# Dilated attention of the prompt: keys by remainder and one softmax for three groups, in one inference step of a hybrid sparse decoder

## The chip, the cores and the metric

One Trainium2 chip, one of its cores. The metric is the device time of one execution of the whole program, in microseconds; lower is better. The five engines of the core are TensorE (PE in the profile; PEld are its weight loads), VectorE (DVE), ScalarE (ACT), GpSimd (POOL) and SyncE (SP), which here only issues DMA transfers.

## What is computed

One layer over a prompt of 512 tokens and a sample group of 8 sequences with 4 new tokens each and 2048 tokens of past: RMS norm, one wide projection, two attention mixers, a gated merge, a mixture of experts. The change is in the second mixer for the prompt, dilated attention with three groups of four heads of 64:

```python
DIL_CONFIGS = ((128, 1), (512, 4), (2048, 16))     # (window, dilation)

def dilated_prompt(q, k, v, window, dil):           # per group; residues() sorts tokens by position % dil
    span = window // dil
    ...
    mask = (m_k >= 0) & (diff >= 0) & (diff <= span)
    p, lse = masked_softmax(s, mask)
    o = jnp.einsum('brnhqk,brnkhe->brnqhe', p, vw)

def combine_dilations(outs, lses):
    w = jax.nn.softmax(jnp.stack(lses, axis=-1), axis=-1)
    o = jnp.einsum('bthn,bthnd->bthd', w, jnp.stack(outs, axis=-2))
```

A query of group 0 reads itself and the 128 keys behind it, one of group 1 every 4th key behind it, one of group 2 every 16th. The three outputs of a head are weighted by a softmax over the groups' log denominators. That is the same as one softmax over the keys of all three groups together.

The outputs also hold the updated window caches: for the sample group each is the old cache moved on by four tokens (a copy from HBM to HBM, here called a cache move) with the new rows at its end.

## The kernel before

The program is a sequence of blocks; each is a list of instructions per engine, ordered by semaphores, and a block begins when the one before has ended on all engines.

- `norm_and_project` (L180): projection. A loop of turns takes two chunks of 328 columns of the weights. `load` (L217) loads a chunk on SyncE when TensorE has finished with its buffer, VectorE splits it in two parts, TensorE multiplies. The loop on SyncE (L223) has four turns of two loads.
- `finish_rows` (L429): merge gates, rotary embedding, compressor. SyncE stores the rows of keys and values to the prompt's caches (`put`, L476) and issues the eight moves of the 512 cache.
- `prompt_nsa` (L777): the first mixer for the prompt, 32 steps of scores, maximum, exponential, turned probabilities, values. SyncE issues two moves of the 2048 cache (4088 KB each) when each of four head pairs begins, and at the end waits until the rows are stored (L967).
- `prompt_dilated` (L1119): the block that changes. 24 steps: 2 head pairs x 4 tiles of 128 queries x 3 groups. `step(k)` (L1134) gives the key blocks of a step: up to 2 for group 0, all up to the diagonal for groups 1 and 2, whose masks (`dil1`, `dil2`) cross out keys with another remainder. `scores` (L1224) forms queries x keys and adds the mask with a product of the identity in bf16 (L1238); `maxima` on VectorE (L1367), `exps` on ScalarE (L1314). When the three groups of a unit have their exponentials, `max_differences`, `group_factors` and `weights` work out one factor for each group and GpSimd multiplies the exponentials (L1209). `turn_probs` transposes them (L1250), `copy_pT` on VectorE (L1388) and ScalarE (L1329) brings them to SBUF, `values` (L1263) multiplies: the values (64 columns) are the stationary operand and 128 queries stream, so the output comes out turned and `copy_o` (L1393) stores it. TensorE's order in iteration k is scores of k + 6, probabilities of k + 1, values of k. Ahead of the loop six turns bring queries and keys of the first pair (L1216); `turn_next` does it for the second. `sample_queries` and `sample_keys_and_gates` prepare the next block within the last four steps.
- On SyncE this block issues the loads of group 1's cached keys and values (g1) for the next block, then, when each head pair begins, four moves of the 128 cache (248 KB each) and four of the window cache (508 KB each), then the first window keys (`load_first_window_keys`, L1471), whose place is in `rows`.
- `sample_dilated` (L1496): the same mixer for the sample group; it begins with g1 and the first window keys. Then come `sample_nsa`, `mix` and `experts`.

An f32 product appears as two MATMUL instructions with a weight load each, a transpose or a bf16 product as one.

## Time and profile before

| what | us |
|---|---|
| three runs, median (lowest to highest) | 1165.11 (1160.56 to 1166.38) |
| profiled execution, span | 1161.6 |
| TensorE busy | 1055.2 (91%) |
| VectorE, ScalarE, GpSimd busy | 501.6, 331.2, 175.6 |
| block of `prompt_nsa` | about 305 to 406 |
| block of `prompt_dilated` | about 406 to 477 |
| `sample_dilated` begins | 478 |
| expert weights in the chain that ended last | 9.5% of the span |

For the profiled execution the page gives the span, from the first to the last instruction; it lies within the three runs. The span is cut in 40 slices of 29 us; TensorE is at 9 tenths in most, the DMA engines above 9 tenths in the last nine but two. A busy TensorE is not one at its peak: pipelined products overlap, and what a group of products costs is read from the starts of the groups. In every view times count from the start of the span.

### The profile page before, as it was taken

To read this page: it belongs to the slowest core of one execution; us is meant where nothing else is said; L and a number is where in the kernel's file an instruction comes from. 1 tells how busy PE (TensorE), PEld (TensorE's weight loads), DVE (VectorE), ACT (ScalarE), POOL (GpSimd) and SP (SyncE) were. 2 spreads that over 40 slices of the span, in tenths; PEclk is the share of its full clock that TensorE was granted. 3 is DMA by queue.
4 is the path that set the end of the run, shared out by engine and by line. 5 is a ranking of instruction groups with operands and counts; after the bars stand their busy time and mean duration, and the time that the engine had idled before them with its cause. 6 is when DMAs were issued, how large, how long until landed. Compare 5 with 4: busy or idle time off the path is not lost. (4 is left out here: it accounts for less than half of the span.)

```text
span 1161.6 us, 20328 instructions
## 1 busy us (share of the span) xinstructions
PE 1055.2 (91%) x8174; PEld 780.8 (67%) x8176; DVE 501.6 (43%) x1065; ACT 331.2 (29%) x766; POOL 175.6 (15%) x212
## 2 busy tenths in 40 slices
PE   6999999999889979886999999999997999888785
PEld 6999999999856646765887887887555433333332
DVE  5444343333367668643656657526216211100105
ACT  4100001221346556422555454520111111100103
POOL 0260000500035534201010010000000112011200
PEclk9999999999869999997999999999998999898989
DMA  8421250887379997497555343409916899999966
GB/s 259 130 90 55 87 147 14 230 307 262 139 254 348 326 307 248 132 340 238 229 198 209 146 171 148 159 1 335 419 69 261 304 425 421 422 424 425 424 258 248
DMA packets 99119, 279.05 MB, mean 240 GB/s; under 512 B 17540, under 2 KB 72736, under 8 KB 87648
## 3 DMA queue, kind: packets, MB, share of 16 engines
q1 hardware_dynamic: 88992, 228.72, 54.7%
q0 software_dynamic: 6976, 42.48, 9.6%
q10 hardware_dynamic: 3072, 6.75, 1.5%
q8 instruction: 55, 0.90, 0.3%
q14 instruction: 24, 0.20, 0.1%
HBM read 263.67 MB, written 69.53 MB: 287 GB/s over the span
## 5 line engine op out<-in xcount | busy, mean ns | idle before, releaser
L3100 PE MATMUL ex_up_ps<-ex_w_up,ex_hT 128*64 128x512 f32 x512 | 123.5, 638 | 27.1 <-DMA ex_w_up<-in_expert_w_up 25.5
L123 PE MATMUL proj_acc<-w_in_upper,hT_upper 128*128 128x328 f32 x352 | 112.3, 319 | 2.6 <-DVE hT_rest L117 2.3
L125 PE MATMUL proj_acc<-w_in_upper,hT_rest 128*128 128x328 f32 x352 | 110.5, 314 | 0.0
L3100 PEld LDWEIGHTS ex_up_ps<-ex_w_up,ex_hT 128*64 128x64 f32 x512 | 41.6, 146 | 97.6 <-issue 86.7
L124 PE MATMUL proj_acc<-w_in_rest,hT_upper 128*128 128x328 f32 x252 | 79.8, 316 | 0.0
L123 PE MATMUL sn_hp<-sn_xT,cmp_w_upper 128*128 128x256 f32 x256 | 76.4, 298 | 0.0
L123 PE MATMUL proj_acc<-hT_upper,merge_w_upper 128*128 128x272 f32 x256 | 74.3, 290 | 1.3 <-ACT qT_dil L557 1.3
L124 PE MATMUL proj_acc<-hT_rest,merge_w_upper 128*128 128x272 f32 x256 | 73.7, 288 | 0.0
L125 PE MATMUL proj_acc<-hT_upper,merge_w_rest 128*128 128x272 f32 x256 | 73.5, 287 | 0.0
L124 PE MATMUL sn_hp<-sn_xT,cmp_w_upper 128*128 128x256 f32 x256 | 73.1, 286 | 0.0
L125 PE MATMUL sn_hp<-sn_xT,cmp_w_rest 128*128 128x256 f32 x256 | 73.1, 285 | 0.0
L123 PEld LDWEIGHTS proj_acc<-w_in_upper,hT_upper 128*128 128x128 f32 x352 | 66.7, 189 | 4.5 <-DVE hT_rest L117 2.7
L3254 DVE TENSOR_TENSOR ex_act<-ex_silu,ex_up_ps 128x256 f32<-128x256 f32 x16 | 6.7, 420 | 144.9 <-ACT ex_silu L3190 144.9
L125 PEld LDWEIGHTS proj_acc<-w_in_upper,hT_rest 128*128 128x128 f32 x352 | 66.7, 190 | 0.0
L3123 PE MATMUL ex_down_ps<-ex_w_down,ex_actT 128*64 128x512 f32 x256 | 58.4, 597 | 2.1 <-DMA ex_w_down<-in_expert_w_down 1.4
L123 PEld LDWEIGHTS sn_hp<-sn_xT,cmp_w_upper 128*128 128x128 f32 x256 | 49.3, 193 | 2.2 <-issue 1.9
L1838 POOL DMA_INDIRECT sn_raw<-in_cache_nsa_paged,page_rows x16 | 17.4, 1090 | 215.6 <-ACT sn_v L2233 148.7
L124 PEld LDWEIGHTS sn_hp<-sn_xT,cmp_w_upper 128*128 128x128 f32 x256 | 49.4, 193 | 0.0
L125 PEld LDWEIGHTS sn_hp<-sn_xT,cmp_w_rest 128*128 128x128 f32 x256 | 49.3, 193 | 0.0
L123 PEld LDWEIGHTS proj_acc<-hT_upper,merge_w_upper 128*128 128x128 f32 x256 | 48.1, 188 | 1.7 <-ACT qT_dil L557 1.5
L2199 ACT CAST sn_xT<-sn_tp 128x512 fp32r<-128x512 f32 x64 | 34.3, 591 | 51.7 <-PE sn_tp L2034 41.4
L977 POOL TENSOR_TENSOR qrot_and_spare<-qrot_and_spare,pn_stats 128x256 f32<-128x256 f32 (+3 forms) x32 | 40.1, 1253 | 55.8 <-DVE pn_stats L1045 55.8
(530 smaller groups left out, 2125.7 us busy)
## 6 DMA issues: line engine op xcount, KB each, us to landing
ex_w_up<-in_expert_w_up SPq DMA_DIRECT2D x30, 2048.0 KB, 29.5
ex_w_down<-in_expert_w_down SPq DMA_DIRECT2D x32, 1024.0 KB, 30.1
out_dil_sample<-in_cache_dil_w SPq DMA_DIRECT2D x8, 4088.0 KB, 27.8
sd_kv_g<-in_cache_dil_w SPq DMA_DIRECT2D x32, 512.0 KB, 7.6
w_in_chunk<-in_w_in SPq DMA_DIRECT2D x10, 1312.0 KB, 5.9
merge_w<-in_w_in SPq DMA_DIRECT2D x16, 512.0 KB, 5.7
out_dil_sample<-in_cache_dil_w SPq DMA_DIRECT2D x8, 1016.0 KB, 8.5
merge_gates_scratch<-qT_dil ACTq DMA_DIRECT2D x16, 272.0 KB, 4.5
```

The costliest lines, as they stand in the source:

```text
L123: pe.matmul(out, a[0], b[0], start=first, stop=False)
L124: pe.matmul(out, a[0], b[1], start=False, stop=False)
L125: return pe.matmul(out, a[1], b[0], start=False, stop=last)
L977: pool.tensor_tensor(part, part, bc(st[:, k % 8, 3, :], 2, [P, 2, n]), ALU.mult).then_inc(s_sc, 1)
L1838: pool.indirect_dma_start(self.sn_raw[:, g % RAW].rearrange("c p x -> c (p x)"), None, half, bass.IndirectOffsetOnAxis(ap=self.page_rows[: ...
L2199: act.copy(xT[:, x_units_to(u) % XR, 0, :, bank, 0:P], a[bank][:, :].rearrange("p (j c) -> p j c", j=4)).then_inc(s_ea, 1)
L3100: ins = pe.matmul(up_ps[r, q, :], hT[:, q, c, r], wu[slot][:, u, c, :], start=c == 0, stop=c == KD - 1)
L3123: ins = pe.matmul(dn_ps[r, half, :], aT[:, q, c, r], wd[slot][:, u, c, half * 512:(half + 1) * 512], start=c == 0, stop=c == 1)
L3254: dve.tensor_tensor(ac[:, q, :], sl[:, q, :], up_ps[:, q, FF:2 * FF], ALU.mult).then_inc(s_ac, 1)
```

## The change

- Queries of a tile are ordered by position modulo 4 (`RES`), so 32 queries (`RQ`) have one remainder. For groups 1 and 2 each of the four sets of 32 queries is multiplied with the keys of its own remainder only: (i + 1) x 32 keys for tile i instead of (i + 1) x 128. Group 2 keeps a mask for its steps of 4 within them.
- The scores of all three groups of a unit lie side by side in one PSUM bank per head, at most 256 + 2 x 128 columns, and one maximum, one exponential and one sum serve them all. The factors, the differences and GpSimd's multiplications are gone. There are 8 units instead of 24 steps.
- In `values` the probabilities become the stationary operand and 64 value columns stream. The output comes out with queries as rows: `normalize` divides it by the sum, `turn_output` transposes it, `copy_o` stores it in the old order.
- Groups 1 and 2 need values by remainder; `prompt_nsa` loads them back from the stored caches into `v_turned`, on SyncE ahead of the 2048 moves, after a wait for the stored rows and the turned queries.
- The moves of the 128 cache and the window cache go from this block to the loop of the projection, two of each per turn.
- The sample's copies on ScalarE and VectorE go behind the loop; the mask table shrinks from 1536 to 1152 columns.

```diff
+RES, RQ = 4, P // 4
@@ norm_and_project, SyncE
                         load(0, i + 1)
                         load(1, i + 1)
+                        for j in range(2):
+                            for src, dst in (("cache_nsa_win", "nsa_win_sample"), ("cache_dil_w128", "dil128_sample")):
+                                self.move_cache(sp, src, dst, 2 * i + j)
@@ prompt_nsa, SyncE
+                    sp.wait_ge(s_qt, PAIRS)
+                    sp.wait_ge(self.s_rows_out, 16 * self.n_rows_out)
+                    for g in range(2):
+                        stored = self.o[f"dil{WINDOWS[1 + g]}_prompt"][0, 0].rearrange("(j r) x h d -> j r x (h d)", r=RES)
+                        sp.dma_start(v_turned[:, g], stored[:, :, 1, :]).then_inc(self.s_vt, 16)
                     for c in range(PAIRS):
                         sp.wait_ge(s_s, U * c + 1)
...
-                    sp.wait_ge(self.s_rows_out, 16 * self.n_rows_out)
@@ prompt_dilated, SyncE
-                    for c in range(PAIRS):
-                        sp.wait_ge(s_s, U * c + 1)
-                        for j in range(BS // PAIRS):
-                            for src, dst in (("cache_dil_w128", "dil128_sample"), ("cache_nsa_win", "nsa_win_sample")):
-                                self.move_cache(sp, src, dst, BS // PAIRS * c + j)
+                    sp.wait_ge(s_s, NT + 1)
                     self.load_first_window_keys(sp)
@@ GpSimd
-                    for k in range(N):
-                        c, i, g, kb, n = step(k)
-                        pool.wait_ge(s_co, k // 3 + 1)
-                        part = ex[:, k % EX, :, 0:n]
-                        pool.tensor_tensor(part, part, bc(st[:, k // 3 % 4, 4, g, :], 2, [P, 2, n]), ALU.mult).then_inc(s_sc, 1)
@@ TensorE
+                    def scores(u):
+                        c, i, kb, n0, m = unit(u)
...
+                        heads = [slice(hh * HD, (hh + 1) * HD) for hh in range(2)]
+                        for hh, r in enumerate(heads):
+                            pe.matmul(S[u % 2][:, hh, 0:n0], qT(c, 0)[r, i * P:(i + 1) * P], kT[r, c, 0, k0:k0 + n0], start=True, stop=False)
+                        for g in (1, 2):
+                            at = n0 + (g - 1) * m
+                            for res in range(RES):
+                                q0 = i * P + res * RQ
+                                for hh, r in enumerate(heads):
+                                    pe.matmul(S[u % 2][res * RQ:(res + 1) * RQ, hh, at:at + m], qT(c, g)[r, q0:q0 + RQ],
+                                              kT[r, c, g, res * P:res * P + m], start=False, stop=False)
+                        near, strided = self.mask("near"), self.mask("strided")
+                        s0 = RQ * i * (i + 1)
+                        for hh in range(2):
+                            pe.matmul(S[u % 2][:, hh, 0:n0], self.ident_b[:, :], near[:, 2 * P - n0:2 * P], start=False, stop=False)
+                            ins = pe.matmul(S[u % 2][:, hh, n0:n0 + 2 * m], self.ident_b[:, :], strided[:, s0:s0 + 2 * m], start=False, stop=True)
...
+                    def values(u):
...
+                        for hh in range(2):
...
+                            for a, b in enumerate(kb):
+                                pe.matmul(O[u % 2][:, hh, :], pT[:, u % 2, 0, hh, a * P:(a + 1) * P], rows[:, b, v:v + HD], start=a == 0, stop=False)
+                            for g in range(2):
+                                for res in range(RES):
+                                    at = g * P + res * RQ
+                                    ins = pe.matmul(O[u % 2][res * RQ:(res + 1) * RQ, hh, :], pT[0:m, u % 2, 1, hh, at:at + RQ],
+                                                    v_turned[0:m, g, res, h * HD:(h + 1) * HD], start=False, stop=g == 1)
...
+                    for u in range(-2, N):
+                        if u + 2 < N:
+                            scores(u + 2)
+                        if u >= 1:
+                            turn_output(u - 1)
+                        if 0 <= u + 1 < N:
+                            turn_probs(u + 1)
+                        if u == N - 1:
                             sample_queries()
...
+                        if u >= 0:
+                            values(u)
+                        if 0 <= u + 1 < 3:
+                            turn_next(u + 1)
+                    turn_output(N - 1)
```

## Rows read from the trace of the kernel before

**Rows 1.** Which piece of the chain that ended last: start us, us, what

```profile
966.80 33.52 DMA ex_w_up<-in_expert_w_up
```

**Rows 2.** Windows: us, busy us by engine (x instructions), granted clock, DMA share, GB/s

```profile
320.00:325.00 5.00, 5.00 (x38) 3.74 (x36) 1.82 (x3) 0.00 (x0) 0.00 (x0) 0.50 1.24 422
...
340.00:345.00 5.00, 5.00 (x46) 2.81 (x40) 4.20 (x12) 3.54 (x10) 2.77 (x3) 1.00 0.01 3
...
405.00:420.00 15.00, 10.56 (x87) 6.72 (x84) 9.34 (x30) 7.73 (x32) 5.09 (x10) 1.00 0.99 332
...
440.00:460.00 20.00, 19.61 (x175) 12.25 (x175) 15.40 (x48) 12.41 (x48) 9.80 (x10) 1.00 0.83 267
...
460.00:480.00 20.00, 16.71 (x180) 13.14 (x178) 13.27 (x36) 9.97 (x34) 10.21 (x8) 1.00 0.01 3
```

**Rows 3.** Timeline at both ends of the dilated block: start us, us, engine, line

```profile
409.25 0.49 PE L1234 MATMUL pd_S<-qrot_and_spare,rows 64*128 64x128 f32 x4
...
409.36 0.58 ACT L1344 COPY qrot_and_spare<-pd_O 128x512 f32<-128x512 f32 x1 [0.29 <-PE pd_O L1216]
...
476.05 0.22 DVE L1415 TENSOR_REDUCE gate_rows<-sq_gates 128x6 f32<-128x48 f32 x1
```

**Rows 4.** Timeline of TensorE in a dense stretch of the dilated block

```profile
442.78 0.70 PE L1234 MATMUL pd_S<-qrot_and_spare,rows 64*128 64x256 f32 x4
443.42 0.39 PE L1238 MATMUL pd_S<-masks_bf,ident_bf 128*128 128x256 bf16 x2
443.64 1.04 PE L1250 MATMUL pd_PT<-ident,pd_exp 128*128 128x128 f32 x8
444.61 0.66 PE L1263 MATMUL pd_O<-qrot_and_spare,rows 128*64 128x128 f32 x8
445.20 0.70 PE L1234 MATMUL pd_S<-qrot_and_spare,rows 64*128 64x256 f32 x4
...
447.03 1.09 PE L1263 MATMUL pd_O<-qrot_and_spare,rows 128*64 128x128 f32 x16
448.05 0.70 PE L1234 MATMUL pd_S<-qrot_and_spare,rows 64*128 64x256 f32 x4
```

**Rows 5.** Timeline of TensorE, groups with few weight columns or few streamed, later blocks

```profile
486.31 1.08 PE L1630 MATMUL sd_Sd<-sd_kT,sd_qTz 128*32 128x128 f32 x32
...
502.91 1.42 PE L1600 MATMUL sd_Sd<-sample_place,qT_dil 128*128 128x32 f32 x12
...
512.28 0.40 PE L1670 MATMUL sd_O<-sample_place,sd_pTn 32*32 32x128 f32 x8
...
639.84 2.38 PE L2096 MATMUL sn_misc<-sn_v,sn_pT 128*32 128x128 f32 x40
```

**Rows 6.** Groups by line, 405 to 480 us: busy us, mean ns, idle before

```profile
L1209 POOL TENSOR_TENSOR pd_exp<-pd_exp,pd_stats 128x512 f32<-128x512 f32 x10 | 10.2, 1039 | 27.0 <-DVE pd_stats L1381 27.0
...
L1367 DVE TENSOR_REDUCE pd_stats<-pd_S 128x2 f32<-128x1024 f32 x4 | 4.9, 1220 | 1.1 <-PE pd_S L1238 1.0
```

**Rows 7.** Timeline of SyncE's DMA issues: start us, us, line, transfer

```profile
66.24 64.11 SPq L219 DMA_DIRECT2D w_in_chunk<-in_w_in  x5
...
275.35 2.15 SPq L478 DMA_DIRECT2D out_dil_sample<-rows  x3
...
406.46 24.84 SPq L1494 DMA_DIRECT2D sd_kv_g<-in_cache_dil_w  x8
...
442.62 11.85 SPq L1476 DMA_DIRECT2D rows<-in_cache_nsa_win  x4
```

**Rows 8.** Timeline of VectorE in the projection

```profile
88.05 1.53 DVE L113 CAST w_in_upper<-w_in_chunk 128x2624 fp32r<-128x2624 f32 x1 [4.87 <-DMA w_in_chunk<-in_w_in]
...
91.39 1.17 DVE L117 TENSOR_TENSOR w_in_rest<-w_in_chunk,w_in_upper 128x984 fp32r<-128x984 f32 x1
```

**Rows 9.** DMA issues by line: count, KB each, median us to landing

```profile
out_nsa_win_sample<-in_cache_nsa_win SPq DMA_DIRECT2D x8, 508.0 KB, 9.0
```

**Rows 10.** Waits of SyncE: who waited for whom, us in total, times, longest

```profile
SPq L649 <- PE pn_S L868: 68.2, 4, 29.8
```

## What the change was predicted to do

> **What bounds the kernel now.** I read the chain of work that ended last first. It reaches back only to 882.87 us and from 966.8 us on it is mostly expert weights in transit [rows 1]; nothing in it lies in the stage that changes. But that stage is one link of a sequence of blocks, and the transfers that end the kernel are issued in buffers that come free only after the blocks before. So I take a microsecond saved in the dilated block as a microsecond saved at the end, unless a transfer that the next block needs isn't there. Second, the windows [rows 2]: in 440 to 460 us TensorE is busy 19.6 of 20 us, VectorE 15.4, ScalarE 12.4, GpSimd 9.8. So this block is TensorE's when it is full, and it is not full at its start: 10.6 of 15 us from 405 to 420. Third, the block's ends [rows 3]: first scores at 409.25, last step (the gates) over at 476.3 us.
>
> **What TensorE's work costs.** The dense stretch [rows 4] gives each group by start-to-start. Scores of 256 keys: 0.64 us. Masks of 256: 0.22 for two, nothing lost before the transposes. Eight transposes: 0.97. Value products: 8 instructions 0.59, 16 instructions 1.02, so 54 ns per instruction of 128 columns plus 0.15 per group. 54 ns is 128 columns at about one a cycle of 2.4 GHz. So the 0.64 is 4 instructions x 107 ns plus 0.21, and a transpose is some 0.105 with 0.13 per group. A step with n key blocks costs 0.49 + 0.75n. Before has 24 steps with 54 key blocks: 24 x 0.49 + 54 x 0.75 = 52.3 us.
>
> After has 8 units. An f32 product is two instructions, and the kinds are these:
> - Near scores, masks, transposes (6 in the first unit of a head pair, 8 in the others) and the turn of the output (one transpose, 0.1) go by the prices above.
> - Scores by remainder: 16 products with 32 query columns, 32 instructions per unit, over 32, 64, 96 or 128 keys.
> - Near values now load 128 weight columns and stream 64. The nearest row is L1600 (128 columns loaded, 32 streamed): 12 instructions in 1.42 us, 0.114 us each [rows 5]. So 0.46 us per head with two key blocks, where the old form took 0.22.
> - Values by remainder: 16 products, 32 instructions per unit, 32 weight columns, 64 streamed.
>
> The price of those 512 small instructions isn't in the trace, and it is the largest unknown. Rows with 32 weight columns [rows 5]: L1630, rotating over four column groups, 26 ns at 128 columns streamed (1.08 us less 0.27 for the last one, by 31); L1670, 19 ns; L2096, with two groups taking turns, 54 ns, which is its stream. The values rotate over four groups like L1630, so 27 ns. The scores use two heads on one group before they move on, like L2096, so I take the larger of 27 ns and their stream: 27, 27, 33 (partly overlapped), 40 ns by unit. Bounds: 19 ns and 54 ns.
>
> Unit by unit (near scores + remainder scores + masks + output turn + transposes + values): first 0.42 + 1.07 + 0.24 + 0.1 + 0.8 + 1.9 = 4.6; second 0.64 + 1.07 + 0.34 + 0.1 + 1.0 + 2.4 = 5.6; third 0.64 + 1.27 + 0.39 + 0.1 + 0.9 + 2.4 = 5.7; fourth 0.64 + 1.49 + 0.44 + 0.1 + 0.8 + 2.4 = 5.9. (Values: per head 0.46 near + 0.15 + 16 x 27 ns + 0.15; 0.23 near in the first unit. The 0.2 more in the transposes of the first two is for outputs narrower than the array.) Sum 21.8, both pairs 43.5 us. So TensorE's own work falls by 8.8 us only: three groups of steps are gone, but the remaining keys come in small pieces.
>
> **The waits.** Before, the loop takes 66.3 us (409.25 to 475.6) with 52.3 of this work and 4.9 of turns for the second pair and for the sample (same in both), so 9.1 us are stalls, nearly all in the slow filling seen in rows 2. They come from the combination of groups: a unit's probabilities can't be turned until three steps of exponentials, the factors and GpSimd's multiplications are through. After, a unit needs one maximum (up to 1.22 us, [rows 6]) and two exponentials, and GpSimd's 24 multiplications (1.0 us each at 512, [rows 6]) are gone; they were beside TensorE and are worth only the fill. Following the new order by hand, the first unit waits some 1 us for its exponentials and 1 us for the copies before the next turn; I take 3.5 us. So 5.6 us saved. Against it: the first scores wait for the copies of all three groups, 409.9 instead of 409.25 (ScalarE's third copy starts at 409.36 and takes 0.58, [rows 3]), 0.7 us; and the tail now multiplies, turns and copies after the last product, 0.9 us more. The sample's copies move behind the loop but run beside the last values. VectorE per unit: 1.22 + 0.2 maxima, about 0.5 normalizing, 0.3 output copy, 0.7 probability copy, 2.9 us against 5.9 of TensorE; ScalarE about 2.1. Both are hidden.
>
> 8.8 + 5.6 - 0.7 - 0.9 = 12.8, **13 us saved**.
>
> **The transfers.** The next block needs its first keys. SyncE issues the g1 loads from 406.5 to 431.3 and the first window keys from 442.6 to 454.5 [rows 7], behind 6.3 MB of small cache moves. The DMA engines rest from 460 on (share 0.01, [rows 2]). With the moves gone, the window keys are issued when the fifth unit is scored (near 432), and the work left in the queue, about 1 MB behind g1, lands near 440, while the block now ends at 463. Hidden, with 20 us to spare. The new value loads (1 MB) wait on SyncE in front of the 4 MB cache moves: for stores that were issued by 277.5 us [rows 7] and for the queries to be turned, which the moves wait for in any case. They delay the first moves by about 3 us (1 MB at the 320 GB/s of the stage), which the hole at 340 to 345 us (DMA share 0.01) absorbs [rows 2].
>
> The small moves (8 of 508 KB [rows 9] and 8 of 248 KB) go behind a weight load in the projection: 1.5 MB in each of four turns, about 5 us. They stand on SyncE ahead of the next turn's loads, whose turn comes 16 us later. Loads are issued every 16 us (five issues from 66.24 to 130.35, [rows 7]), so one goes out near 82.3; it has landed at 88.05 and is split by 92.6 [rows 8], and its chunk begins near 98. So there are 5 us of slack even if the moves shared the engines with the load ahead of them. Cost 0; 0 to 4 us as bounds, none of it likely. The smaller mask table saves nothing, TensorE doesn't wait there.
>
> **A rule that speaks against the change.** The group overhead of 0.15 to 0.21 us in rows 4 appears wherever the shape of the array's use changes; before that is 3 times in each of 24 steps, after 6 or 7 times in each of 8 units, so 72 against about 54. The Trainium skill says the same of the cause (TensorEngine Tiling (Array Packing), Key Properties: changing the tiling mode drains the engine), and the new unit switches back and forth between heads in its values. The overhead is in my sum.
>
> **Rivals.**
> - The small pieces run at the two-group pace everywhere. 54 ns for all 512 instead of 29 on average is +12.6 us: no gain, 1165. Against it: the values rotate like L1630.
> - The small pieces overlap fully. A unit uses eight different places of the array (two halves of its rows, four quarters of its columns). Were all eight streaming at once, an instruction would cost an eighth of 54 ns, 7 ns: 512 x 22 ns = 11 us more, 24 saved, 1141. The rows speak against it: four groups give 26 and 19 ns, not 13 or less [rows 5]. By the Trainium skill (TensorE: Matmul & The Clock Gate, Part 3, The mechanism) tiles in different places start about 4 ns apart; by that rule the pieces would be as cheap as in this rival; the trace doesn't agree for f32 products.
> - The stalls stay. If the fill and the alternation of engines cost 9 us as before, the saving is 7: 1158.
> - Slower: the clock. The granted clock is 0.50, which is the lower level of 1.2 GHz, in 320 to 325 us, after a block's start with gaps [rows 2]. The first head pair of the attention before, of which two thirds lie in that stretch, kept SyncE waiting 29.8 us; the other three waits sum to 38.4, of which one is the short first, so 19 us for a later pair [rows 10]. Two thirds at the lower level cost a half more, so the whole some 70%. The loop's 52 us would be some 35 longer: 1165 - 13 + 35 = 1187. It decides from a third of the loop at the lower level (13 of 35). For it: the new loop also begins with gaps, and no row shows pieces of 64 x 32 in a long series. Against it: the old fill had TensorE busy 10.6 of 15 us and kept 1.00 [rows 2], and the new one has fewer gaps.
>
> **How the numbers follow.** The profiled execution spans 1161.6 us, the three runs are 1160.56 to 1166.38 with median 1165.11; I subtract from the median: 1165.1 - 13 = 1152. Chances: forecast (8 to 17 saved) 0.60, stalls stay 0.13, two-group pace 0.12, full overlap 0.05, half clock 0.10. Within 0.5% is 5.8 us, which is about what a measurement of this kernel can tell from no change. Faster: 0.60 + 0.05 + half of the stalls case = 0.70. Same: the other half, most of the two-group case: 0.18. Slower: 0.12. The range holds forecast, stalls and two-group cases, and at the low end 19 ns pieces (-5 us) and the spread of runs (3 us): 1144 to 1167.
>
> **What would show it.** In the profile after: the dilated block from about 406 to 463 us instead of 476. Groups of 32 instructions of 32 columns in about 1.1 us (right) or 1.9 (two-group pace). Near values at 0.11 us an instruction. First value products near 420 us. The window keys land before 445 us. The projection's windows still 20.00 of 20. Granted clock 1.00 in the block. The expert stage as long as before. I am wrong if small instructions cost 50 ns, if a clock below 1 stands in the block, or if TensorE waits for keys behind it.

## The result and the profile after

The changed kernel takes 1146.07 us in the median of 4 executions (1142.88 to 1149.66) against 1165.13 us of the kernel before (1160.56 to 1166.38, 4): the ratio is 0.9846 with a 95% interval of 0.9825 to 0.9867, so it is 19 us or 1.5% faster. In later comparisons the same two kernels stood at 0.9837 (0.9791 to 0.9883), 0.9828 (0.9791 to 0.9865) and 0.9828 (0.9798 to 0.9859). Over all 20 executions of the changed kernel the median is 1145.8 us, and they lie between 1139.94 and 1151.17. The first four runs of before lie within 6 us, but all its 48, with those of the later comparisons, spread as widely, from 1160.12 to 1173.26 (9 to 13 us on each of the later chips); so the 11 us of the changed kernel are not by themselves a sign of the change. What they come from is asked below.

The profiled execution took 1149.66 us, of which the span is 1147.8; it is the slowest of its four. Its chain of work that ended last is of the same kind as [rows 1] (start, us, what):

```profile
966.23 37.83 DMA ex_w_up<-in_expert_w_up
```

The windows that answer [rows 2], with those between 420 and 440 us added (us, busy us of TensorE, its weight loads, VectorE, ScalarE, GpSimd with counts, then granted clock, DMA share, GB/s):

```profile
320.00:325.00 5.00, 5.00 (x34) 3.40 (x32) 2.16 (x3) 0.00 (x0) 0.00 (x0) 0.50 1.04 399
340.00:345.00 5.00, 5.00 (x50) 3.03 (x46) 4.20 (x12) 3.85 (x10) 3.36 (x2) 1.00 0.63 213
405.00:420.00 15.00, 11.74 (x210) 9.35 (x209) 7.43 (x15) 6.81 (x18) 3.33 (x7) 1.00 0.95 317
420.00:425.00 5.00, 3.10 (x50) 2.16 (x48) 1.61 (x4) 0.61 (x2) 0.00 (x0) 0.94 0.89 289
425.00:430.00 5.00, 5.00 (x50) 4.41 (x49) 1.81 (x4) 1.92 (x5) 0.00 (x0) 0.50 1.07 346
430.00:435.00 5.00, 4.23 (x53) 3.57 (x53) 2.07 (x6) 0.58 (x1) 0.00 (x0) 0.50 0.70 224
435.00:440.00 5.00, 5.00 (x79) 3.69 (x77) 1.05 (x3) 1.40 (x5) 0.00 (x0) 0.50 0.74 207
...
440.00:460.00 20.00, 19.04 (x341) 15.77 (x325) 11.19 (x35) 8.47 (x28) 0.00 (x0) 0.93 0.01 3
460.00:480.00 20.00, 15.47 (x167) 13.03 (x167) 11.05 (x30) 5.91 (x15) 2.69 (x2) 0.78 0.57 171
```

GpSimd is out of the loop, VectorE and ScalarE have become lighter, and the block is TensorE's. But the granted clock, which the forecast had at 1.00 all through the block, is at 0.50 (the lower level, 1.2 GHz) in three windows on end. The ends of the block, for [rows 3]:

```profile
409.29 0.49 PE L1232 MATMUL pd_S<-qrot_and_spare,rows 64*128 64x128 f32 x4 [0.77 <-ACT qrot_and_spare L1355]
...
462.43 0.22 DVE L1433 TENSOR_REDUCE gate_rows<-sq_gates 128x6 f32<-128x48 f32 x1
```

The gates end at 462.65 instead of 476.27: 13.6 us earlier. So this one execution shows just the saving that was forecast, with a clock that wasn't. A second profile of the same kernel (run e1) shows the block with no such stretch. Its gates are at 453.00, 23 us earlier than before, and its span is 1140.4 us. Here is its dense stretch at full clock, for [rows 4] (start us, us, engine, line, shapes, count):

```profile
437.99 0.70 PE L1232 MATMUL pd_S<-qrot_and_spare,rows 64*128 64x256 f32 x4
438.62 0.67 PE L1238 MATMUL pd_S<-qrot_and_spare,rows 64*32 64x128 f32 x32
439.22 0.28 PE L1243 MATMUL pd_S<-masks_bf,ident_bf 128*128 128x256 bf16 x1
...
439.67 0.27 PE L1286 MATMUL pd_O<-ident,pd_o_rows 128*128 128x128 f32 x1
439.77 0.38 PE L1258 MATMUL pd_PT<-ident,pd_exp 128*128 128x128 f32 x2
...
440.65 0.56 PE L1276 MATMUL pd_O<-rows,pd_pT 128*128 128x64 f32 x4
441.13 0.43 PE L1280 MATMUL pd_O<-qrot_and_spare,pd_pT 64*32 64x64 f32 x16
441.49 0.66 PE L1276 MATMUL pd_O<-rows,pd_pT 128*128 128x64 f32 x4
442.08 0.43 PE L1280 MATMUL pd_O<-qrot_and_spare,pd_pT 64*32 64x64 f32 x16
```

L1232 are the near scores, L1238 the scores by remainder, L1243 the masks (with L1244, not shown), L1286 the turn of the output, L1258 and L1260 (not shown) the transposes, L1276 the near values, L1280 the values by remainder. By start-to-start, the 32 instructions of L1238 over 128 keys take 0.60 us, or 19 ns each, where 40 were forecast. (Instructions are counted here, two to each f32 product.) The 16 of L1280 take 0.36 us, or 22 ns, where 27 and a group overhead were. Scores over 32, 64 and 96 keys take 0.29, 0.39 and 0.50 us: 9, 12 and 16 ns.

The maxima of VectorE in the whole block, for [rows 6] (the multiplications of GpSimd are gone):

```profile
L1387 DVE TENSOR_REDUCE pd_stats<-pd_S 128x2 f32<-128x384 f32 (+3 forms) x8 | 7.7, 957 | 14.7 <-PE pd_S L1244 14.7
```

SyncE in the changed kernel, for [rows 7]; the small moves now stand between the weight loads of the projection:

```profile
83.61 0.55 SPq L653 DMA_DIRECT2D out_nsa_win_sample<-in_cache_nsa_win  x1
...
98.84 16.32 SPq L220 DMA_DIRECT2D w_in_chunk<-in_w_in  x2
...
405.67 22.42 SPq L1509 DMA_DIRECT2D sd_kv_g<-in_cache_dil_w  x8
433.49 2.68 SPq L1491 DMA_DIRECT2D rows<-in_cache_nsa_win  x4
```

### The profile page after: what moved, and what is told of

It is laid out like the page before. It is cut to its first block and busy times, and to the rows that moved or that the text cites. A ratio compares the mean times of both kernels' runs of the same rounds, so it can differ in the third digit from the quotient of the medians.

```text
span 1147.8 us, 20576 instructions
## 1 busy us (share of the span) xinstructions
PE 1046.5 (91%) x8408; PEld 782.3 (68%) x8408; DVE 476.7 (42%) x985; ACT 310.8 (27%) x678; POOL 148.2 (13%) x188
## 5 line engine op out<-in xcount | busy, mean ns | idle before, releaser
L125 PE MATMUL sn_hp<-sn_xT,cmp_w_upper 128*128 128x256 f32 x256 | 72.5, 283 | 0.0
L126 PEld LDWEIGHTS proj_acc<-hT_upper,merge_w_rest 128*128 128x128 f32 x256 | 48.3, 189 | 0.0
L125 PEld LDWEIGHTS proj_acc<-hT_rest,merge_w_upper 128*128 128x128 f32 x256 | 48.1, 188 | 0.0
L125 PEld LDWEIGHTS proj_acc<-w_in_rest,hT_upper 128*128 128x128 f32 x252 | 48.1, 191 | 0.0
```

The costliest lines, as they stand in the source:

```text
L125: pe.matmul(out, a[0], b[1], start=False, stop=False)
L126: return pe.matmul(out, a[1], b[0], start=False, stop=last)
```

## The experiments

To compare profiles I use three marks in each: the last output copy of the attention before (`oT<-pn_O`), the gates (`gate_rows`), and the start of the last group of the product `sd_tq<-sample_place,sd_o`, near the end of the block that follows. The marks of before, the last of each kind:

```profile
405.90 0.29 DVE L1064 COPY oT<-pn_O 128x128 f32<-128x128 f32 x1 [0.92 <-PE pn_O L935]
...
546.17 1.03 PE L1681 MATMUL sd_tq<-sample_place,sd_o 128*128 128x16 f32 x4 [1.39 <-DVE sd_o L1800]
```

With the gates of [rows 3] at 476.05 the dilated block is 70.2 us long in before, the next block 70.1, and the rest, which is the span behind the third mark, 615.4. A pause is idle time of TensorE in front of a product in the dilated block which waited for nothing that the profile shows ("issue"); only those over 0.3 us are listed.

| run | executions | median us (range) | ratio to before (95%) | dilated block | pauses, us | next block | rest |
|---|---|---|---|---|---|---|---|
| changed kernel, first profile | 4 | 1146.07 (1142.88-1149.66) | 0.9846 (0.9825-0.9867) | 57.3 | 0.92, 1.90 | 70.2 | 615.1 |
| e1 changed kernel | 4 | 1144.32 (1142.25-1149.93) | 0.9837 (0.9791-0.9883) | 47.4 | none | 71.2 | 616.2 |
| e10 changed kernel | 6 | 1143.58 (1139.94-1151.17) | 0.9828 (0.9791-0.9865) | 49.0 | 0.75 | 71.3 | 615.3 |
| e12 changed kernel | 6 | 1147.74 (1140.65-1150.75) | 0.9828 (0.9798-0.9859) | 53.0 | 1.79 | 71.1 | 618.6 |
| e2 moves back | 4 | 1147.55 (1144.65-1154.97) | 0.984 (0.9799-0.9882) | 56.6 | 3.44, 1.76 | 72.5 | 618.8 |
| e3 before, moves only | 10 | 1163.67 (1159.66-1169.22) | 0.9988 (0.9967-1.001) | 70.2 | none | 69.7 | 615.6 |
| e4 no 2048 moves | 4 | 1141.08 (1138.9-1142.19) | 0.9793 (0.9754-0.9832) | 46.9 | none | 71.5 | 613.7 |
| e5 busy end | 5 | 1146.08 (1142.16-1148.04) | 0.9817 (0.9789-0.9845) | 52.3 | 2.32, 0.75 | 70.9 | 616.0 |
| e6 late moves | 5 | 1145.88 (1144.74-1146.72) | 0.9828 (0.9805-0.985) | 48.0 | none | 74.5 | 613.7 |
| e7 heads outer | 4 | 1144.81 (1144.22-1146.63) | 0.9814 (0.9788-0.984) | 49.8 | 0.94 | 73.0 | 615.9 |
| e8 scores twice | 4 | 1154.94 (1151.81-1157.26) | 0.9909 (0.9882-0.9937) | 59.3 | 2.43, 1.92, 0.80 | 70.5 | 614.3 |
| e9 early moves | 6 | 1140.62 (1139.67-1143.88) | 0.9801 (0.9771-0.983) | 47.7 | none | 72.8 | 613.7 |
| e11 early moves | 5 | 1141.93 (1140.1-1143.54) | 0.979 (0.9764-0.9816) | 46.9 | none | 72.1 | 616.6 |

e1 to e4 ran on one chip, e5 to e8 on another, e9 with e10, and e11 with e12. A comparison within a group needs no detour over the kernel before. The changed kernel did not run beside e5 to e8. The rest lies between 613.7 and 618.8 us, so some 5 us of a profile's time come from behind the two blocks; what makes them is not shown. Behind each median stand 4 to 10 executions, behind each row of blocks and pauses one.

### e1: the changed kernel again

> The changed kernel once more, unaltered. Theory: 13.6 us of the saving are made in the dilated block (ends 462.65 instead of 476.3 in its first profile) and the rest is spread between runs, so the time is 1143 to 1150, 15 to 22 below before, and the profile shows again a stretch of 10 to 20 us at granted clock 0.50 between 415 and 445 us and two pauses of 0.9 and 1.9 us inside the remainder scores. Rival: the stretch at 0.50 and the pauses are chance, and a second profile shows 1.00 from 405 to 455 and the block ending near 452, with a time near 1137.

The rival came true for the profile, and the theory for the time: this execution has no pause and no stretch at the lower clock, and its block is 47.4 us. The other three are at 1142.56, 1146.09 and 1149.93 us. So the first profile is not what the kernel always does, and what has to be explained is a difference between executions of one program.

### e2 and e3: the small cache moves

e2 is the changed kernel with the moves back in the dilated block; e3 is the kernel before with nothing but the moves changed. The diff is that of e2 in the dilated block, where the same moves leave the projection.

```
-                    sp.wait_ge(s_s, NT + 1)
+                    for c in range(PAIRS):
+                        sp.wait_ge(s_s, NT * c + 1)
+                        for j in range(BS // PAIRS):
+                            for src, dst in (("cache_dil_w128", "dil128_sample"), ("cache_nsa_win", "nsa_win_sample")):
+                                self.move_cache(sp, src, dst, BS // PAIRS * c + j)
```

> The new attention with the small cache moves put back into the dilated block. Theory (moves cost nothing in the projection, and in the block they only delay the window keys, of which the block has 20 us to spare): within 3 us of the changed kernel, and TensorE's pauses in the fill stay as they are. Rival: the gain beyond the 13 us forecast comes from the transfers taken out of the block; then it is 5 us or more slower than the changed kernel, and the next block waits for its keys.

> The kernel before with the small cache moves alone put into the projection. Theory: within 1 us of before, projection windows still 20.00 of 20 busy, all of the saving belongs to the attention. Rival: the moves are worth 4 to 6 us by themselves (the part of 19 that 13 doesn't explain), so 1159 to 1161.

e3: 0.9988 with 1 inside the interval, so the moves alone bring 1.4 us with bounds of 4 and -1, and the gain is the attention's. e2 is 3.2 us above e1, with intervals that cover each other; the limit of 3 us in the expectation was missed by a hair. Its profile has the longest pause of all, 3.44 us, and a second of 1.76 in the last unit, behind the same 21st of 32 instructions as the pause of e10 in the table; the expectation saw neither coming.

```profile
446.77 0.44 PE L1239 MATMUL pd_S<-qrot_and_spare,rows 64*32 64x128 f32 x11 [1.76 <-issue]
```

With the transfers back, more of them are queued while the block runs (DMA share 0.92 to 1.05 from 440 to 450 us, where the changed kernel has 0.02).

### e4: without the moves of the 2048 group

```
-                    for c in range(PAIRS):
-                        sp.wait_ge(s_s, U * c + 1)
-                        for j in range(BS // PAIRS):
-                            self.move_cache(sp, "cache_dil_w2048", "dil2048_sample", BS // PAIRS * c + j)
```

> The changed kernel without the cache moves of the 2048 group (32 MB less traffic; that output is left out). It asks what makes the two pauses inside the remainder scores and the fall of the clock behind them. Theory: the pauses are the fetch of instructions (a 16 KB instruction packet lies at 409 and at 420 us, where the pauses are) behind the bulk transfers; with the engines of the DMA nearly idle they shrink from 0.9 and 1.9 us to under 0.3, the granted clock stays 1.00 to 455 us, and the block takes 43 to 47 us from first scores to its end instead of 53. Rival 1: the pauses go but the clock falls all the same, since it falls for the small pieces themselves: 50 us. Rival 2: the pauses stay, for the fetch takes as long without traffic: 53 us. The total time may fall more for other reasons, since the moves are missing from all that follows.

This kernel leaves the cache of the 2048 group out of its output. No pause, the clock at 1.00 until 450 us, a block of 46.9 us, and four executions within 3.3 us. This is the theory's case, with a caution that e1 gives: one profile without a pause can be chance. The first profile of the changed kernel shows why I looked here. The remainder scores of units two and four:

```profile
410.91 0.41 PE L1238 MATMUL pd_S<-qrot_and_spare,rows 64*32 64x64 f32 x21
412.25 0.33 PE L1238 MATMUL pd_S<-qrot_and_spare,rows 64*32 64x64 f32 x11 [0.92 <-issue]
...
421.00 0.29 PE L1238 MATMUL pd_S<-qrot_and_spare,rows 64*32 64x128 f32 x1
423.19 0.67 PE L1238 MATMUL pd_S<-qrot_and_spare,rows 64*32 64x128 f32 x31 [1.90 <-issue]
```

TensorE stops in the middle of a group whose operands and semaphores are all there. The transfers in two slices of 0.2 us, 409.4 to 409.6 and 420.8 to 421.0 us, by queue (packets, MB, share of the engines):

```profile
q1 hardware_dynamic: 2, 0.07, 103.8%
q8 instruction: 1, 0.02, 43.3%
...
q1 hardware_dynamic: 29, 0.03, 50.8%
q8 instruction: 1, 0.02, 29.6%
```

Each pause ends 2.2 to 2.8 us after such a 16 KB packet of instructions began: 2.8 and 2.4 here, 2.5 and 2.5 in e2 (412.47, goes on at 414.94, and 444.25, goes on at 446.77), 2.2 and 2.6 in e5, 2.6 in e7, 2.3 to 2.6 in e8, 2.5 in e10, 2.6 in e12 (411.63, goes on at 414.23). In each of the six profiles with a pause whose loop has the same products, a break stands where another profile has one too: behind the 21st of 32 over 64 keys in the first profile, e2 and e12, behind the 1st over 128 in the first and e5, behind the 21st over 128 of the last unit in e2, e7 and e10. A stop in front of fixed instructions, of varying length, soon after a late packet of instructions: that is a fetch. The Trainium skill has the mechanism (Runtime: NRT & Kernel Launch, Instruction fetch mechanics): each engine's instructions come through a buffer refilled in blocks of 16 KiB, 256 instructions, by a DMA queue of the engine's own. The size of the packets agrees.

So does the count. I numbered TensorE's records in the order of time (products, weight loads and its sequencer's; a few can be missing). All pauses of the table, in all profiles, stand in front of record 7385, 7642, 7897, 8154 or 8410, give or take one: 256 apart. e8 is the sharpest case, for its loop has 256 more products' instructions and as many weight loads. (Its whole profile has 59 packets of 16 KB on this queue instead of 57, so two more for 512 records, where the expectation under e8 speaks of four.) There record 7642 is in the middle of the group over 96 keys and not at the start of the one over 128, and the pause stands before it all the same:

```profile
419.88 0.62 PE L1238 MATMUL pd_S<-qrot_and_spare,rows 64*32 64x96 f32 x33 [2.43 <-issue]
```

The packets are late as well. In e4, with the DMA engines nearly idle, TensorE passes record 8410 at 439.21 us and a packet begins at 439.38; it passes 8666 at 447.72, and the next begins at 447.83. In the first profile, with the bulk queued, it passes record 7129 at 401.77 us and the packet begins at 409.48, 7.7 us later; record 7385 at 412.25, and the packet begins at 420.83, 8.6 us later. Each of these two packets is followed by a pause in front of the next such place. In e1 record 7129 is passed at 402.25, the packet begins at 407.89, 5.6 us later, and record 7385 follows without a pause at 411.53. So a packet is asked for one block of 256 ahead, waits behind the transfers, and TensorE stops when it runs through the block in less time than that. The skill's page also says that the fetch is hidden because issuing is slower than the refill; with the bulk queued it is not hidden here, in a loop that takes 5 to 9 us for 256 records.

### e5: TensorE kept busy at the block's end

`fill(n, out)` is n bfloat16 products of identity and mask whose results are never read.

```
+                        if u == N - 1:
+                            fill(6, S[0][:, 0, 0:2 * P])
                         if u >= 1:
                             turn_output(u - 1)
...
+                            fill(4, S[0][:, 0, 0:2 * P])
                             sample_queries()
...
+                    fill(8, PT[:, 0, 0:2 * P])
                     turn_output(N - 1)
+                    fill(8, PT[:, 0, 0:2 * P])
```

> The changed kernel with 26 bfloat16 products of identity and mask (256 columns, 0.107 us each at full clock, results never read) put where TensorE waits at the end of the dilated block: 6 ahead of the turn of the output before last, 4 ahead of the sample's transposes, 8 ahead of and 8 behind the last turn. Theory: the clock falls to 0.50 near 448 (or 458) us because TensorE waits and runs only small transposes there, and stays there into the next block (last values 1.10 us instead of 0.59, L1607 at 0.23 us each instead of 0.11); with the fill the clock stays 1.00 to 475 us, which gives back 1.5 us in this block and 2 to 3 in the next against 1 us for the fill: 2 to 4 us below the changed kernel, and the mean granted clock of a run up by 0.006. Rival: the clock falls there whatever TensorE does (both traces of the changed kernel show it at the same step), and the time is 0 to 1.5 us above the changed kernel.

Neither came out clearly. The clock still fell, before 455 us; it was back at 0.97 in the window from 460 us, which holds the next block's first products. The next block took 70.9 us against 71.2 in e1 and 73.0 in e7. The dilated block took 4.9 us more than in e1; 3.1 are its two pauses, 1.8 are left for the fill. In the median it is 1.3 us above e7, which has no fill, and 0.2 above e6. The theory's 2 to 4 us are not there. With the transfers as the changed kernel has them the next block takes 70.2 to 73.0 us after the new loop against 70.1 after the old one, which bounds what the fall at the end costs there at 0 to 3 us; how to avoid it stays open.

### e6: the bulk moved behind the block

```
+                    sp.wait_ge(s_s, NT)
                     for part in range(2):
                         self.load_cache(sp, "g1", 0, part)
                     sp.wait_ge(s_s, NT + 1)
                     self.load_first_window_keys(sp)
+                    for b in range(BS - 2, BS):
+                        self.move_cache(sp, "cache_dil_w2048", "dil2048_sample", b)
```

The loop of `prompt_nsa` issues the other six, by the condition shown under e9.

> The changed kernel, all of its output, with the g1 loads held until the fourth unit is scored, the window keys behind them, and the last two of the eight 4 MB moves of the 2048 group behind those. It thins the transfers at 400 to 420 us, where TensorE paused in its fetch of instructions. Theory: the pauses come from instruction packets that stand behind bulk transfers; no pause over 0.3 us in the remainder scores, the clock 1.00 until 445, and all runs like the quickest of the changed kernel (1142 to 1143) at mean clocks of 0.956 or more, where five of its eight were at 1145 to 1150 with 0.950 to 0.953: 2 to 3 us below its median. Rival 1: the pauses are no matter of transfers, then the same spread as the changed kernel. Rival 2: the two moves now reach into the next block's loads (467 to 475 us) and it is 3 to 8 us slower.

Both the theory's mechanism and rival 2 came true. There is no pause over 0.3 us (the longest is 0.27, before record 8154), and the block is 48.0 us; but the two moves keep the DMA engines at 0.88 to 1.03 from 445 to 465 us, and the next block, which lives on its loads, takes 74.5 us instead of 71.2. Against before the ratio is 0.9828, like the changed kernel's on other chips (0.9828 to 0.9846), with a spread of 2.0 us. The pauses had been traded for a wait.

### e7 and e8: what a small product costs

e7:

```
-                            for res in range(RES):
-                                q0 = i * P + res * RQ
-                                for hh, r in enumerate(heads):
+                            for hh, r in enumerate(heads):
+                                for res in range(RES):
+                                    q0 = i * P + res * RQ
```

and e8:

```
-                                for hh, r in enumerate(heads):
+                                for hh, r in 2 * list(enumerate(heads)):
```

> The changed kernel with the remainder scores in another order: four remainders of one head, then four of the other, so that consecutive products rotate over four column groups in one half of the rows. It measures what the forecast took wrongly. In the changed kernel's order 32 instructions take 0.28, 0.45, 0.49 and 0.60 us (9 to 19 ns each) for 32 to 128 keys. Theory: two row halves and four column groups all overlap, and a piece costs what its weight load costs, not its stream; in the new order two pieces on the same rows share no half, so the 128-key group takes 26 ns an instruction as in L1630 of before (0.83 us or more), the whole 1 to 1.5 us slower. Rival: the column groups alone carry the overlap, then 0.60 us as before and no change.

> The changed kernel with every remainder score product issued twice (256 more instructions of TensorE, the scores by remainder doubled, so part of the output is changed). It prices a small instruction against the end of the block. Theory A (9 to 19 ns a piece at full clock): the remainder groups take 0.55 to 1.2 us instead of 0.28 to 0.60, together 3.9 us more in the eight units, so 4 us above the changed kernel where nothing pauses; since four more packets of instructions are fetched, pauses of 1 to 3 us and the half clock behind them come more often, and the median is 5 to 10 us above. Rival B (27 to 40 ns a piece, the forecast): 8 us more, the groups 1.7 to 2.5 us long.

e7, over 128 keys, at full clock:

```profile
421.10 0.67 PE L1238 MATMUL pd_S<-qrot_and_spare,rows 64*32 64x128 f32 x32
421.70 0.28 PE L1243 MATMUL pd_S<-masks_bf,ident_bf 128*128 128x256 bf16 x1
```

0.60 us for the 32, to the hundredth what the other order takes. The theory falls: the order of heads and remainders doesn't matter, and the 26 ns of L1630 [rows 5] were no floor for products on one half of the rows. The stream of such an instruction is 54 ns, so on average nearly three of them are under way at once. e8:

```profile
446.00 1.23 PE L1238 MATMUL pd_S<-qrot_and_spare,rows 64*32 64x96 f32 x64
447.16 0.28 PE L1243 MATMUL pd_S<-masks_bf,ident_bf 128*128 128x256 bf16 x1
...
450.51 1.44 PE L1238 MATMUL pd_S<-qrot_and_spare,rows 64*32 64x128 f32 x64
451.88 0.28 PE L1243 MATMUL pd_S<-masks_bf,ident_bf 128*128 128x256 bf16 x1
```

64 take 1.16 and 1.37 us, 18 and 21 ns each; the second 32 cost 0.66 and 0.77 us where the first cost 0.50 and 0.60, so the groups are somewhat longer than I expected, and far from the 1.7 to 2.5 of the forecast's price. The block has three pauses with 5.2 us together, and the time is 10 us above e7, at the upper end of theory A's 5 to 10: about half of it are the products (0.66 and 0.77 us more in the two groups shown, twice each, and about 0.5 in each of the four shorter ones, 4.9 in all), the rest is the fetch and the clock (0.58 and 0.74 from 435 to 445 us).

### e9 to e12: the bulk moved ahead of the block

e9 and e11 are one kernel, with all of the output. Two of the eight 4 MB moves are issued where the DMA engines had nothing to do, and the other six stay.

```
                     for m in range(MERGE_RING):
                         self.load_merge_w(sp, m)
+                    for b in range(BS - 2, BS):
+                        self.move_cache(sp, "cache_dil_w2048", "dil2048_sample", b)
                     tables_loaded(sp)
...
                         for j in range(BS // PAIRS):
-                            self.move_cache(sp, "cache_dil_w2048", "dil2048_sample", BS // PAIRS * c + j)
+                            if BS // PAIRS * c + j < BS - 2:
+                                self.move_cache(sp, "cache_dil_w2048", "dil2048_sample", BS // PAIRS * c + j)
```

> The changed kernel, all of its output, with two of the eight 4 MB moves of the 2048 group issued at the end of the projection, behind the first loads of the merge weights (the DMA engines rest there from 180 to 200 us), and six left where they were. The bulk of the moves is then through by 390 us instead of 415, and nothing is pushed into the next block. Theory: TensorE's pauses in the remainder scores come from instruction packets behind that bulk; no pause over 0.3 us, the dilated block 47 to 48 us from the last output of the attention before to its gates (47.4 without a pause, 49.8 to 57.3 with), the next block 71 to 73 us, all runs at 1141 to 1144, 2 to 3 us below the changed kernel of the same chip. Rival 1: pauses come and go whatever the transfers do, so the spread of the changed kernel. Rival 2: the two moves stand in front of the merge weights or the stored rows and make the stages at 200 to 315 us 2 us or more longer, which takes the gain away.

> The changed kernel unaltered on the same chip, as the other end of the comparison and as a third profile of it. Theory: 1145 in the median, between 1142 and 1150, with a pause in the remainder scores in half of its runs or more; if its profile has a pause, the instruction packet in front of it lies 2.4 to 2.9 us before TensorE goes on, as at 409.4 and 412.25, and the block is 50 us or longer; if it has none, the block is 47 to 48 us. Rival: a pause with no instruction packet ahead of it, or at another instruction than the 21st and 22nd or the first and second of a group of 32, which would take the ground from the reading as a fetch.

> The kernel of e9 (two of the 4 MB moves issued at the end of the projection) once more, since the intervals of e9 and e10 overlap (0.9801 and 0.9828, each some 0.003 wide to either side). Theory: early transfers take the pauses away, so again a median near 1141, all runs within 5 us of each other and none above 1145, no pause over 0.3 us in the profile. Rival: e9 was lucky; then its runs spread over 8 us or more like those of the changed kernel (1140 to 1151 in 14 runs) and the profile has a pause.

> The changed kernel unaltered beside e11 on the same chip. Theory: median 1144 to 1146, spread of 7 us or more, 2 to 4 us above e11 in the median, and a pause in the profile in more cases than not (2 of its 3 profiles so far). Rival: median within 1 us of e11.

The windows of e9:

```profile
400.00:405.00 5.00, 4.72 (x56) 3.25 (x56) 2.68 (x12) 1.98 (x8) 1.23 (x2) 1.00 0.01 3
405.00:420.00 15.00, 12.68 (x222) 9.83 (x230) 8.43 (x18) 7.36 (x19) 3.35 (x7) 1.00 0.86 277
420.00:440.00 20.00, 19.23 (x407) 15.80 (x406) 10.83 (x27) 7.52 (x22) 0.00 (x0) 1.00 0.20 59
440.00:450.00 10.00, 9.03 (x138) 7.80 (x138) 6.09 (x24) 5.26 (x20) 0.00 (x0) 0.87 0.01 2
450.00:455.00 5.00, 2.16 (x23) 1.54 (x23) 1.41 (x7) 0.53 (x3) 0.68 (x1) 0.50 0.00 0
```

The bulk is through by 395 us (the expectation had 390). TensorE passes record 7129 at 401.50, as in the first profile, but now the packet begins at 401.72 and not 7.7 us later. The clock is 1.00 until 447 us, and TensorE has 19.23 of 20 us from 420 to 440. Against before the two comparisons give 0.9801 and 0.979, and beside the changed kernel on the same chip it is 3.0 and 5.8 us faster in the median. The intervals against before overlap with the changed kernel's in both; it is the two comparisons together that speak for it (means 3.1 and 4.8 us lower; were the runs shuffled within each chip, so large a sum would come up some 3 times in 1000). Its 11 executions lie within 4.2 us (1139.67 to 1143.88), the 20 of the changed kernel within 11.2.

Of e10's expectation the place of the pause holds (440.54, behind the 21st of 32, with the packet at 438.0), but its block is 49.0 us, not 50 or more, and its runs reach from 1139.94 to 1151.17 instead of 1142 to 1150. e12 has its pause behind the 21st too (414.23), and its clock is at 0.50 from 415 to 420 us; its median is 1147.74 where 1144 to 1146 were expected, 5.8 above e11 instead of 2 to 4. Of that profile's time 2 us more than in e11 lie in the rest, which the moves don't explain.

Taken together: of 8 profiles with the full bulk queued at 400 to 415 us and the new loop (four of the changed kernel, e2, e5, e7, e8) seven have a pause; of 4 with it thinned (e4, e6, e9, e11) none has. The pauses are the fetch of instructions behind bulk transfers. The kernel before has the late packets too, but not the pauses: it passes record 7129 at 402.56 us (give or take some missing records), the packet begins at 409.33, and TensorE is at record 7385 only at 421.8. Its packets begin at 409, 426, 444, 455 and 467 us, 11 to 18 us apart, the first profile's from 409 on 6 to 11. So waits of some 4 to 7 us are over in the kernel before when the instructions are needed, and in the new loop they are not. I ran no kernel that varies the rate alone; e8, with the most instructions, has the most pauses.

That the spread of the executions comes from the pauses is less sure. The kernels with the bulk thinned spread over 2.0 to 4.2 us, but e7 has a pause in its profile and spreads over 2.4, and the kernel before has none and spreads over 13.

The clock is less settled. All four blocks with a stretch at the lower clock before their end (first profile, e2, e8, e12) have a pause of 1.79 us or more, and none of the blocks without a pause has such a stretch. In the first profile the fall follows the pause of 1.90 us, in e2 and e12 it comes within the pause, and in e8 it follows the pause of 0.80. But e5 paused for 2.32 us and stayed at 1.00, and so did e2 at its second pause and e8 at its first two. So in these runs a pause begins before each such fall, and isn't enough for one.

## Why the prediction was right, and where its numbers were off

**Direction, range and size.** Faster was right, and 1146.07 lies in 1144 to 1167. The point, 13 us saved, was 6 too few, and that it came so near is in part luck: the work fell by 11.5 us more than forecast, and pauses, clock and a slower next block, which the forecast didn't have, took some of it back. The block alone saves 22.8 us where nothing disturbs it (70.2 to 47.4, e1); the pauses and the clock take 2 to 10 back in three of its four profiles (49.0, 53.0, 57.3), and the next block 0 to 1.

**What TensorE's work costs** is the step that was mis-sized. Forecast were 43.5 us for the eight units. At full clock e1 has these, in the order of the forecast's list: 0.42 + 0.29 + 0.27 + 0.11 + 0.65 + 1.35 = 3.1; 0.63 + 0.39 + 0.34 + 0.11 + 0.87 + 1.79 = 4.1; 0.63 + 0.50 + 0.39 + 0.11 + 0.87 + 1.79 = 4.3; 0.63 + 0.60 + 0.45 + 0.11 + 0.87 + 1.79 = 4.5. Sum 16.0, both pairs 32: 11.5 less than forecast. The 512 small instructions hold most of it. Scores by remainder are 2 x 1.78 = 3.6 us where 9.8 were forecast, values by remainder 16 x 0.36 = 5.8 where 9.3 were, so 9.3 instead of 19.1. They cost 9 to 22 ns instead of 27 to 40, and the group overhead of 0.15 to 0.2 us wasn't added to them. The rest is in the near values and transposes. The near values' price from L1600 was nearly right: 4 instructions in 0.48 and 0.59 us, 0.12 to 0.15 each with their overhead against 0.61 per head forecast. The 0.2 us allowed for transposes with narrow outputs, for which no row stood, weren't there: 0.65 us for six and 0.87 for eight, 0.11 each, in all units.

The forecast's rule, the larger of 27 ns and the stream, gives 40 and 54 ns for 96 and 128 keys; it put 33 and 40 in their place without a row, and even these were twice what was measured. The reason for the 40 ns was the comparison with L2096, "two heads on one group before they move on". e7 shows that this order costs nothing. The lower bound of 19 ns, L1670, was the nearest row after all for the longest pieces, and shorter streams cost less than any row of before.

**The balance.** Work 52.3 - 32 = 20.3. Stalls: e1's loop runs from 409.77 to 451.55, 41.8 us, less 4.9 of turns and 32 of work, and less some 1.2 for its last values at the lower clock: 3.7 us, where 3.5 were forecast, 5.4 saved. Start: 4.2 us from the last output copy to the first scores against 3.35, so 0.8 lost (forecast 0.7). Tail: 1.7 us from the last value product to the end of the gates against 0.7, so 1.0 lost (forecast 0.9). 20.3 + 5.4 - 1.2 - 0.8 - 1.0 = 22.7, and the marks say 22.8. The stalls are what is left of the loop when the rest is taken off, so the sum closes nearly by construction; measured on their own are the start, the tail and the 1.2. With that said, three of the four terms were right to 0.2 us, and the 1.2 us of last values at the lower clock had no term.

**The first value products** came at 418.01, forecast near 420.

**Transfers.** The window keys are issued at 433.49 and land before 440, as forecast (near 440, before 445). The projection's windows are 20.00 of 20 from 60 to 180 us in the changed kernel, and e3 bounds the whole of the moves at 4 us gained to 1 lost. The moves that were in [rows 9] land sooner in their new place:

```profile
out_nsa_win_sample<-in_cache_nsa_win SPq DMA_DIRECT2D x8, 508.0 KB, 6.6
```

The new value loads are absorbed: 340 to 345 us has a DMA share of 0.63 where it was 0.01 [rows 2], and TensorE is as busy.

**What the forecast didn't have** is the fetch. It priced instructions by TensorE's time alone, and asked nowhere from where so many would come.

**The rivals.** The clock rival, at 0.10, was half right: the lower level stood in the loop for 17 us of 53 in the first profile (424.4 to 441.5), near the third from which it was to decide, and in the windows from 410 to 425 us in e12. The forecast had named a clock below 1 in the block as a sign that it is wrong, and on this point it was. It didn't make the kernel slower, for TensorE's work had become 11.5 us cheaper than forecast, and it cost some 7 us there (57.3 against 47.4 in e1, less the two pauses). Full overlap (0.05, 7 ns, 24 saved, 1141) gave the better time: an undisturbed execution is at 1140 to 1143. Its price was too low, though, at 9 to 22 ns measured; the time fits because the group overhead and the price of the near values fell too. The Trainium skill's rule beside it (TensorE: Matmul & The Clock Gate, Part 3, The mechanism), about 4 ns from tile to tile, isn't borne out; nor is the same page's floor of some 25 ns from start to start (Part 1, Wait — 56ns, not 53.3ns?) for products in different parts of the array, which these rows go below. The two-group pace (54 ns) and the stalls that stay are refuted by the rows above.

## What to carry to other kernels

Take the price of small products that use different parts of the array from a row with the same number of weight columns and as short a stream, and let an order of theirs be tried before it is feared. When a change packs more instructions into a microsecond, look at what is queued for the DMA engines at that time, for the instructions come the same way; look for "issue" pauses in the middle of a group and for the instruction packets before them, and send bulk where both the engines of the DMA and the instruction stream are at rest. And profile a kernel more than once before its profile is explained, and run the kernel it is compared with as often: the kernel before looked steady in four executions and wasn't in 48.

## What the runs showed of the hardware

- Instructions of f32 products (two to a product) of 64 rows by 32 columns start 9 ns apart at 32 streamed columns, 12 at 64, 16 at 96 and 19 at 128; of 32 to 128 rows by 32 columns with 64 streamed 22 ns (e1). Order among heads and column groups: no difference (e7, 0.60 us for 32 in both).
- TensorE stopped for 0.75 to 3.44 us between two products in 7 of 8 profiles with bulk transfers queued, each time 2.2 to 2.8 us after a 16 KB packet of instructions began, and at places 256 recorded instructions apart. With the DMA engines idle such a packet began 0.1 to 0.2 us after TensorE had passed such a place (e4, e9), with bulk queued 7.7 and 8.6 us after it (first profile). With 8 MB of bulk moved to an idle stretch some 210 us earlier it didn't stop, and the kernel ran at 0.9801 and 0.979 of before instead of 0.9828: the best version with all of the output.
- At the end of the block, with small transposes and waits, the granted clock fell to 0.50 in every profile of the new loop, and 26 filling products (e5) didn't hold it.
